# Chunks of the modulation product moved from the norm stages into local attention

## What is computed

```python
silu_c, silu_cc = silu(c), silu(c_ctx)
for layer in range(2):
    m_lat = split(silu_c @ w_ada[layer] + b_ada[layer], 6)      # w_ada: 1024 x 6144 per layer
    m_ctx = split(silu_cc @ w_ada[layer] + b_ada[layer], 6)
    p = (norm(h) * (1 + m[1]) + m[0]) @ w_in[layer]             # input norm, input projection
    y = concat(gla(p), diff_attention(p), local_attention(p)) @ w_out[layer]
    h = layer_norm(alpha * h + m[2] * y)
    u = norm(h) * (1 + m[4]) + m[3]
    h = layer_norm(alpha * h + m[5] * ((silu(u @ w_g) * (u @ w_u)) @ w_d))
```

## Time and profile before

| what | us |
|---|---|
| median of three runs | 4350.0 |
| lowest and highest run | 4348.49, 4350.08 |
| profiled execution, own time | 4350.14 |
| its span, first to last instruction | 4348.3 |
| TensorE busy | 3612.2 (83%) |
| VectorE busy | 1709.8 (39%) |
| ScalarE busy | 1302.4 (30%) |
| POOL busy | 1244.5 (29%) |

### The profile page before, as it was taken

How to read it: one execution, slowest core, us unless ns; L and a number is a source line. 1 busy time by engine, 2 the same in 40 slices (tenths; PEclk the granted TensorE clock), 3 DMA queues, 4 the chain that set the end, 5 groups by cost and what they waited for, 6 DMA issues and landing times. The chain is left out here.

```text
span 4348.3 us, 51203 instructions
## 1 busy us (share of the span) xinstructions
PE 3612.2 (83%) x19354; PEld 2888.2 (66%) x19354; DVE 1709.8 (39%) x2549; ACT 1302.4 (30%) x2242; POOL 1244.5 (29%) x883
## 2 busy tenths in 40 slices
PE   6899596986686999999994699596958769999991
PEld 2588485764475888888881387485745658888881
DVE  2104453885563121121126304555955622212215
ACT  2211373664433111101103211374745321111111
POOL 1211341212344323323323211341213343333331
PEclk8899697897897999999997799697979879999996
DMA  8322313004332111111106322212032311111112
GB/s 288 146 87 107 98 25 73 19 11 97 95 100 70 39 34 43 39 34 43 39 15 209 128 90 108 83 30 69 15 77 53 130 65 49 43 53 48 43 39 92
DMA packets 150909, 318.16 MB, mean 73 GB/s; under 512 B 11816, under 2 KB 72200, under 8 KB 150768
## 3 DMA queue, kind: packets, MB, share of 16 engines
q1 hardware_dynamic: 128016, 260.20, 19.4%
q10 hardware_dynamic: 18528, 41.97, 2.6%
q0 software_dynamic: 4224, 14.09, 1.2%
HBM read 250.20 MB, written 66.03 MB: 73 GB/s over the span
## 5 line engine op out<-in xcount | busy, mean ns | idle before, releaser
L2027 POOL TENSOR_TENSOR ffn_wlo<-ffn_raw,ffn_whi 128x1024 fp32r<-128x1024 f32 x132 | 314.6, 2391 | 799.9 <-ACT ffn_whi L1998 799.9
L2091 DVE TENSOR_TENSOR ffn_hid<-ffn_up,ffn_silu 128x512 f32<-128x512 f32 (+1 forms) x110 | 70.2, 638 | 1048.6 <-PE ffn_up L127 1022.4
L1998 ACT CAST ffn_whi<-ffn_raw 128x1024 fp32r<-128x1024 f32 x132 | 136.4, 1049 | 944.7 <-PE ffn_acc L127 467.4
L2096 DVE TENSOR_TENSOR y<-ffn_acc,y 128x512 f32<-128x512 f32 x396 | 273.9, 692 | 266.7 <-PE ffn_acc L127 266.7
L125 PE MATMUL ffn_gate<-second_uhi,ffn_whi 128*128 128x512 f32 (+1 forms) x880 | 325.6, 370 | 37.3 <-POOL ffn_wlo L2027 37.3
L126 PE MATMUL ffn_gate<-second_ulo,ffn_whi 128*128 128x512 f32 (+1 forms) x880 | 325.2, 370 | 0.0
L127 PE MATMUL ffn_gate<-second_uhi,ffn_wlo 128*128 128x512 f32 (+1 forms) x880 | 325.0, 369 | 0.0
L126 PE MATMUL ffn_up<-second_ulo,ffn_whi 128*128 128x512 f32 (+1 forms) x880 | 323.9, 368 | 0.0
L125 PE MATMUL ffn_up<-second_uhi,ffn_whi 128*128 128x512 f32 (+1 forms) x880 | 323.8, 368 | 0.0
L127 PE MATMUL ffn_up<-second_uhi,ffn_wlo 128*128 128x512 f32 (+1 forms) x880 | 323.7, 368 | 0.0
L125 PE MATMUL ffn_acc<-ffn_whi,ffn_hhi 128*128 128x512 f32 x792 | 308.2, 389 | 0.0
(11 more groups left out here) (267 smaller groups left out, 8503.0 us busy)
## 6 DMA issues: line engine op xcount, KB each, us to landing
ffn_raw<-w_ffn_dram SPq DMA_DIRECT2D x132, 512.0 KB, 3.5
in_raw<-w_in_dram SPq DMA_DIRECT2D x42, 512.0 KB, 3.6
norm_input_ada_w<-w_ada_dram SPq DMA_DIRECT2D x10, 2048.0 KB, 8.4
norm_ffn_ada_w<-w_ada_dram SPq DMA_DIRECT2D x8, 2048.0 KB, 8.8
proj_scratch<-in_stage ACTq DMA_DIRECT2D x20, 640.0 KB, 2.9
ada_w<-w_ada_dram SPq DMA_DIRECT2D x6, 2048.0 KB
gla_kq<-proj_scratch SPq DMA_DIRECT2D x32, 320.0 KB
swa_qhl<-heads_scratch SPq DMA_DIRECT2D x36, 256.0 KB
```

Of the source, the lines that this page charges most:

```text
L1998: act.copy(whi[:, j % 3, :], raw[:, j % 3, :]).then_inc(w_hi, 1)
L2027: pool.tensor_tensor(wlo[:, j % 3, :], raw[:, j % 3, :], whi[:, j % 3, :].bitcast(F32), ALU.subtract).then_inc(w_ready, 1)
L2091: dve.tensor_tensor(hf[:, c, 0:tn], UP[:, c, 0:tn], sg[:, c, 0:tn], ALU.mult).then_inc(mul_done, 1)
L2096: dve.tensor_tensor(Y[:, tt, cols], ACC[:, half, :], Y[:, tt, cols], ALU.add).then_inc(y_added, 1)
```

## The change

`modulation` does four chunks, 0 to 3 of layer 0. `chunked` is off, so that the norms do none. The other twenty are done inside local attention: in layer 0 chunks 4 to 11 of layer 0 and 0 to 3 of layer 1, shared out over the ten tiles as 0, 0, 1, 1, 2, 2, 2, 2, 1, 1; in layer 1 chunks 4 to 11 of that layer, one for each of the eight tiles. TensorE does the chunk of tile b in the first slot of the tile's first group in `turn`, ahead of the transposes (a second one two slots on), as 32 matmuls of 128 columns on four column groups with a stationary operand of 32 columns (`cs`, of which 2 hold values), into the output bank that the tile will weigh into later. SP loads the first four chunks behind the queries of tile 1, later ones behind the queries of a tile. VectorE adds in one instruction, ScalarE's queue stores in four.

```diff
--- before.py
+++ after.py
@@ -143,7 +143,7 @@
         w_in = [sem(f"ada_w_in{s}") for s in range(4)]
         product_done, row_done = sem("ada_product_done"), sem("ada_row_done")
         row_out = [sem(f"ada_row_out{s}") for s in range(4)]
-        chunks = [(0, c) for c in range(4)] + [(1, c) for c in range(2, 4)]
+        chunks = [(0, c) for c in range(4)]
         block = ctx.enter_context(nc.Block())
 
         def part(c, j):
@@ -251,7 +251,7 @@
             staging = [h[:, 0, :], h[:, 1, :], x[:, 0, :], x[:, 1, :]]
             NS = len(staging)
         TR = ps(nm + "tr", [P, 2, KT, P])
-        chunked = modulated and not attn
+        chunked = False
         MUL, BIAS = 1, 2
         first_chunks = 0 if kind == "input" else 1
         if chunked:
@@ -1398,6 +1398,11 @@
         pr = sb(nm + "p", [P, RING, J, SWA_KEYS])
         pT = sb(nm + "pT", [P, PTS, BANK])
         oT = sb(nm + "oT", [P, 2, BANK])
+        AR = 4
+        W = sb(nm + "ada_w", [P, AR, KT, BANK])
+        B = sb(nm + "ada_b", [P, AR, P])
+        R = sb(nm + "ada_rows", [P, AR, P])
+        cs = sb(nm + "ada_c", [P, KT, 32])
         SC = ps(nm + "scores", [P, 2, 2 * BANK])
         TR = ps(nm + "tr", [P, 2, BANK])
         O = ps(nm + "o_acc", [P, 2, BANK])
@@ -1408,10 +1413,27 @@
         sarg_done, es_done, den_done, rden_done, p_done = sem("sarg_done"), sem("es_done"), sem("den_done"), sem("rden_done"), sem("p_done")
         turned, act_copied, dve_copied, pv_done, o_done = sem("turned"), sem("act_copied"), sem("dve_copied"), sem("pv_done"), sem("o_done")
         stored = [sem(f"stored{s}") for s in range(2)]
+        c_set, product_done, row_done = sem("c_set"), sem("product_done"), sem("row_done")
+        w_in = [sem(f"ada_w_in{s}") for s in range(AR)]
+        row_out = [sem(f"ada_row_out{s}") for s in range(AR)]
         block = ctx.enter_context(nc.Block())
         VG = [(0, 4), (4, 4), (8, 3)]
         LOCAL = N_CTX + 256
         heads = t["heads"]
+        if layer == 0:
+            chunks = [(0, c) for c in range(4, ADA_CHUNKS)] + [(1, c) for c in range(4)]
+            shares = [0, 0, 1, 1, 2, 2, 2, 2, 1, 1]
+        else:
+            chunks = [(1, c) for c in range(4, ADA_CHUNKS)]
+            shares = [1] * len(tiles)
+
+        def chunks_at(b):
+            first = sum(shares[:b])
+            return range(first, first + shares[b])
+
+        def chunk_of(m, c):
+            b, k = m // 2, c // 2
+            return sum(shares[:b]) + k if m % 2 == 0 and 0 <= m < NG and k < shares[b] else None
 
         def by_act(x):
             return x % 5 in (1, 3)
@@ -1446,15 +1468,42 @@
                 rows = slice(64 * half, 64 * half + 64)
                 sp.dma_start(khh[rows, :, :].bitcast(F32), heads[0, HEAD_SK:HEAD_SK + P, :].rearrange("(g p) n -> p g n", p=64)).then_inc(k_in, 16)
                 sp.dma_start(kll[rows, :, :].bitcast(F32), heads[1, HEAD_SK:HEAD_SK + P, :].rearrange("(g p) n -> p g n", p=64)).then_inc(k_in, 16)
+            def load_chunk(n):
+                l, c = chunks[n]
+                if n >= AR:
+                    sp.wait_ge(product_done, n - AR + 1)
+                    sp.wait_ge(row_done, n - AR + 1)
+                cols = slice(c * BANK, (c + 1) * BANK)
+                sp.dma_start(W[:, n % AR, :, :], t["w_ada"][l].rearrange("(k p) n -> p k n", p=P)[:, :, cols]).then_inc(w_in[n % AR], 16)
+                for j in range(4):
+                    part = slice(c * BANK + j * P, c * BANK + (j + 1) * P)
+                    sp.dma_start(B[32 * j:32 * j + 2, n % AR, :], t["b_ada"][l:l + 1, part].to_broadcast([2, P])).then_inc(w_in[n % AR], 16)
+
+            sp.wait_ge(c_set, 2)
             for b, tile in enumerate(tiles):
                 if b >= 2:
                     sp.wait_ge(scores, (b - 1) * H)
                 for part in range(2):
                     sp.dma_start(qhl[64 * part:64 * part + 64, b % 2, :, :].bitcast(F32),
                                  heads[part, HEAD_SQ:HEAD_SQ + 4 * P, tile * P:(tile + 1) * P].rearrange("(a p) n -> p a n", p=64)).then_inc(tile_in[b % 2], 16)
+                if b == 1:
+                    for n in range(AR):
+                        load_chunk(n)
+                if b >= 2:
+                    for n in chunks_at(b - 2):
+                        if n + AR < len(chunks):
+                            load_chunk(n + AR)
+            for b in (len(tiles) - 2, len(tiles) - 1):
+                for n in chunks_at(b):
+                    if n + AR < len(chunks):
+                        load_chunk(n + AR)
 
         @block.gpsimd
         def _(pool):
+            pool.memset(cs[:, :, :], 0.0).then_inc(c_set, 1)
+            pool.memset(B[:, :, :], 0.0).then_inc(c_set, 1)
+            pool.wait_ge(c_set, 2)
+            pool.tensor_copy(cs[:, :, 0:2], res["silu_c"][:, :, :]).then_inc(c_set, 1)
             pool.dma_start(vT[:, :], t["proj"][T_SV * P:(T_SV + 1) * P, :]).then_inc(v_in, 16)
             pool.dma_start(sink[:, :], t["swa_sink"][layer:layer + 1, :].to_broadcast([P, H])).then_inc(sink_in, 16)
             pool.dma_start(bias[:, :, :], t["swa_bias"].rearrange("a p n -> p a n")).then_inc(bias_in, 16)
@@ -1508,6 +1557,8 @@
                 last = c == key_tiles[2 * b] - 1
                 if c == 0 and b >= 2:
                     pe.wait_ge(o_done, b - 1)
+                if c == 0 and shares[b]:
+                    pe.wait_ge(row_done, chunks_at(b)[-1] + 1)
                 pe.wait_ge(act_copied, copies(first_turn[2 * b + 1] + c, True))
                 pe.wait_ge(dve_copied, copies(first_turn[2 * b + 1] + c, False))
                 for g in range(2):
@@ -1516,10 +1567,26 @@
                     mm = pe.matmul(O[rows, b % 2, :], V[:, key_tile(2 * b, c), rows], pT[:, x % PTS, :], start=(c == 0), stop=last)
                 mm.then_inc(pv_done, 1)
 
+            def modulation_chunk(b, n):
+                pe.wait_ge(w_in[n % AR], 80 * (n // AR + 1))
+                pe.wait_ge(c_set, 3)
+                if b >= 2:
+                    pe.wait_ge(o_done, b - 1)
+                k = n - chunks_at(b)[0]
+                if k:
+                    pe.wait_ge(row_done, n)
+                for kt in range(KT):
+                    for j in range(4):
+                        mm = pe.matmul(O[32 * j:32 * j + 32, b % 2, k * P:(k + 1) * P], cs[:, kt, :], W[:, n % AR, kt, j * P:(j + 1) * P],
+                                       start=(kt == 0), stop=(kt == KT - 1))
+                mm.then_inc(product_done, 1)
+
             for s in range(len(slots)):
                 n, j, m, c = slots[s]
                 if j < units_of(n):
                     score(n, j)
+                if c % 2 == 0 and chunk_of(m, c) is not None:
+                    modulation_chunk(m // 2, chunk_of(m, c))
                 if c < turns_of(m):
                     turn(m, c)
                 _, _, m, c = slots[max(s - 2, 0)]
@@ -1558,6 +1625,13 @@
                 if b >= 2:
                     act.wait_ge(stored[b % 2], 32 * (b // 2))
                 act.copy(oT[:, b % 2, :], O[:, b % 2, :]).then_inc(o_done, 1)
+
+            def store_chunk(n):
+                l, c = chunks[n]
+                act.wait_ge(row_done, n + 1)
+                for j in range(4):
+                    part = slice(c * BANK + j * P, c * BANK + (j + 1) * P)
+                    act.dma_start(t["mod"][l, :, part], R[32 * j:32 * j + 2, n % AR, :]).then_inc(row_out[n % AR], 16)
 
             def store(b):
                 tile = groups[2 * b][1]
@@ -1581,6 +1655,11 @@
                     sink_weight(n - 1)
                 if j == 3 and 0 <= n - LAG - 1 and (n - LAG - 1) % 2:
                     store((n - LAG - 1) // 2)
+                _, _, m, c = slots[max(s - 2, 0)]
+                if s >= 2 and c % 2 == 0 and chunk_of(m, c) is not None:
+                    store_chunk(chunk_of(m, c))
+            for s in range(AR):
+                act.wait_ge(row_out[s], 64 * len(chunks[s::AR]))
             for s in range(2):
                 act.wait_ge(stored[s], 32 * ((NG // 2 + 1 - s) // 2))
 
@@ -1626,6 +1705,13 @@
                     dve.wait_ge(pv_done, weighed_before(x - PTS))
                 dve.tensor_copy(pT[:, x % PTS, :], TR[:, x % 2, :]).then_inc(dve_copied, 1)
 
+            def row(b, n):
+                k = n - chunks_at(b)[0]
+                dve.wait_ge(product_done, n + 1)
+                if n >= AR:
+                    dve.wait_ge(row_out[n % AR], 64 * (n // AR))
+                dve.tensor_tensor(R[:, n % AR, :], O[:, b % 2, k * P:(k + 1) * P], B[:, n % AR, :], ALU.add).then_inc(row_done, 1)
+
             for s in range(len(slots)):
                 n, j, _, _ = slots[s]
                 if j == 2 and 1 <= n <= NG:
@@ -1637,6 +1723,8 @@
                     sink_argument(n - 1)
                 if s >= 1 and c < turns_of(m) and not by_act(first_turn[m] + c):
                     take(m, c)
+                if s >= 1 and c % 2 == 0 and chunk_of(m, c) is not None:
```

(1 more changed line is left out.)

## The result

The changed kernel takes 4380.47 us (median of 4 runs, 4376.74 to 4382.86) against 4349.24 us (4346.1 to 4350.08) of the kernel before on the same chip. The ratio is 1.0072, with a 95% interval of 1.0055 to 1.009: 31 us slower. The profiled execution of the kernel after took 4382.86 us, of which 4381.1 is its span; that is 32.8 us more than the span before, and by stage it divides like this.

What follows compares the result with a forecast made beforehand. Limits taken: weight loads in modulation, TensorE in input norm and local attention, VectorE in the later norm. Gains of 29.1 us against costs of 48.7 made net +19.6, so 4370 us, range 4345 to 4396.

Steps and rivals of the forecast that it cites:

- Modulation, 10.96 us: Opening modulation stage, bound by weight loads: two chunks fewer move the last row from 42.22 to 31.26 us, gain 10.96.
- Input norm, 12.8 us: Ten chunks gone: start gains 7.5 us, nine intervals 6.0, last tile loses 0.7; gain 12.8, between 9 and 20.
- the blocked ones: Input norm: two of nine tile intervals lengthened by 2.2 us each by blocked VectorE operations, on top of 7.0.
- the ring: Input norm: loop ScalarE, VectorE, ScalarE, TensorE transposes sets the tile interval once chunks are gone, 7.0 us at low clock.
- Later norm, 5.3 us: Norm behind the first feed-forward network: eight chunks gone, only its start gains, 5.3 us, between 2 and 7.8.
- A chunk in local attention: Sixteen first chunks of a tile cost 2.05 us each, four second ones 1.15 in TensorE's hole; 37.4 us together.
- Queries late behind the weights, layer 0: Local attention: tile 2's queries land behind four chunks' weights; TensorE stalls 8.8 us, plus 1.5 for the low clock.
- The same in layer 1: Local attention, layer 1: tile 2's queries late behind weights; stall 0.7 us, with the clock and spread 1.
- Serial products: Rival, chance 0.03: a chunk's products in local attention run one after another, 7.0 us a chunk, whole 4474 us.
- holes: Rival, chance 0.22: TensorE's holes in local attention take the chunks, 20 us instead of 37.4; whole 4346 or 4336.
- dear chunks: Rival, chance 0.13: wider weights, change of arrangement or ScalarE's stores make each local attention chunk some 3.6 us; whole 4402.
- the point of no gain: Net chunk price below which the whole is faster than before: 0.9 us with late queries, 1.4 without.

Runs made afterwards that it cites:

- Experiment 5: Changed kernel plus sixteen idle 128-column transposes of the identity after each tile's eight in the input norm; 4379.87 us, ratio 1.0079.
- experiment 2: Changed kernel with the chunk of a one-chunk tile two slots later, at the second place; 4367.57 us, ratio 1.0047.
- experiment 1: Changed kernel with the first chunks' weights on SP's queue behind the queries they used to delay; 4363.31 us, ratio 1.0039.

## Why the prediction was right

The forecast was 4370 us with a range of 4345 to 4396, most of the chance on slower; it came out 4380. The mechanism forecast as likeliest is the one that the traces show; the difference to the kernel before was forecast at 19.6 us and is 31.2, so the sizes were short by a third. By its steps:

- **Modulation, 10.96 us:** measured 12.2. Right: the stage with four chunks lasts 34.1 to 36.1 us in the eleven profiles that have it, a gain of 10.3 to 12.4.
- **Input norm, 12.8 us:** measured 9.0. Its start was right (first transposes 7.3 us sooner, 7.5 forecast), the last tile too (0.9 later). The term that was mis-sized is the interval: 7.0 us forecast from the end of the later norm, measured 7.42 to 7.54 (the first 7.23), and the blocked ones 9.4 instead of 9.2. Nine intervals are 70.85 us and not 67.4. That the low clock would come was right, its price was not: 1.97 us for the transposes where the earlier trace rows has 1.75, some 0.2 of the 0.4 us. The other 0.2 is the block in the interval of the earlier trace rows, taken off at 2.2 us where the input norm after has 9.39 - 7.42 = 1.97. Experiment 5 has the ring at 6.65 us with the clock high, so the change gave back 0.9 us a tile of what it had won.
- **Later norm, 5.3 us:** measured 3.1. Its first VectorE step came 2.8 us sooner. The term took the time of a load in the modulation stage for the two megabytes; less than that was on the path, and which of the loads they delayed was not tried.
- **A chunk in local attention:** 2.05 and 1.15 us forecast, 2.04 and 1.21 measured, and the reason for the difference (the second place lies in the hole) is shown by experiment 2. The product with the change of arrangement was put at 1.85 and the rest at 0.2; the starts show 1.98 and under 0.1. The two errors cancel, which is luck. At these prices sixteen and four chunks make 37.5 us (37.4 forecast).
- **Queries late behind the weights, layer 0:** 8.8 us forecast, 12.3 measured; with the low clock 10.3 against 13.1 that experiment 1 took away. Two steps fell short. The weights, at some 386 GB/s, were through 48.0 us after the stage's start and not at 46.7, and then the queries were allowed 1.3 us and took 4.1, at some 200 GB/s: two tiles' worth of them are issued together, in rows of 512 bytes. TensorE wanted them 0.6 us later than forecast.
- **The same in layer 1:** 1.0 us forecast, 4.8 measured by experiment 1. Same cause: here too the weights are through at 48.0 us, and the queries at 54.3. The load of chunk 4, issued 2.6 us behind tile 2's queries, shared the engines with them. The chunk behind the wait ran at the low clock, 3.61 us.
- **Serial products** (7.0 us a chunk, 4474 us), after "TensorE: Matmul & The Clock Gate" of the Trainium skill (Part 3, The mechanism): no. At 32 columns on four groups a chunk of 64 records takes 1.98 us of TensorE. The trace disagrees with the rule as it was read there; the same section also lets a load go ahead when it targets the background weight buffer, which the prediction left out.
- **The other rivals:** holes wanted a chunk at 0.9 us net or less for a gain, and it costs 2.04 or 1.21; dear chunks wanted 3.6, and only the one at the low clock in layer 1 takes that. One sum there is off: without the late queries the point of no gain is 29.1 / 20 = 1.5 us a chunk, not 1.4. Nothing else hangs on it.

The forecast difference was 19.6 us, that of the two spans 32.8. The 13 us between them are 4.5 and 5.0 in the two stages of local attention (the stalls, and first scores 0.6 and 0.5 us later; that the new memsets cause the latter isn't shown, since in layer 1 first scores come 24.2 to 25.3 us after the stage's start without memsets and 24.7 to 25.8 with them), 3.8 and 2.2 in the norms, less 1.2 in modulation and 1.3 in stretches that the change does not touch. These vary between profiles of the same code: from the input norm to local attention it is 835.8 to 843.4 us in the twelve profiles, and the last stretch 982.5 to 987.0. The 2.9 us that the latter lost in the table are of that size, and nothing is concluded from them.

## What to carry to other kernels

Price a piece of work at the engine that sets the pace of the place it goes to: eight chunks cost 3.6 us beside a norm bound by VectorE and 22 in a loop bound by TensorE (9.7 at the best place tried), though the output bank there was idle. Before moving work away from where it is dear, look at its form and its place in the order; here those two together gave 7.5 us where the move gave 9, and charged the other loop nothing. On one queue a bulk load goes behind the small loads that somebody wants sooner: it cost 13 us where weights stood ahead of queries, and with the short product it showed again where weights stood ahead of the residual.

## What was not expected of the hardware

The input norm lost its clock with its filler work: TensorE went to the low level for the whole of the stage (0.50, from 0.90), and sixteen idle transposes a tile brought it back only for part of it (0.69). A record of 128 columns with 32-column weights on four column groups costs 27.2 ns at the high level, no more than with 2-column weights (27 in the earlier trace rows), and entering and leaving that arrangement some 0.2 us. And loads of queries, 256 KB each in rows of 512 bytes, behind 8 MB of weights kept TensorE waiting until 11 us after their issue, 4 of them after the last of the weights, with the DMA engines at some 200 GB/s instead of 386.
